# The kernel table of a state-space branch, built in four 32-column tiles by two row halves of TensorE

## The reference, cut to what matters

```
# u (T, 512) in 32 groups of 16 channels; 64 complex states per group
ab  = exp((a_re + i a_im) * dt)                  # decay of one step
bb  = f * b                                      # (group, state, 16 channels)
h_t = ab * h_(t-1) + bb u_t                      # complex
y_t = Re(c h_t) + d_skip * u_t
```

## Time and profile before

| | us |
|---|---|
| median of 3 runs | 928.42 (928.34 to 928.51) |
| span of the profiled execution, first to last instruction | 926.8 |
| TensorE busy in the span | 912.9 |
| VectorE busy in the span | 603.9 |
| ScalarE busy in the span | 442.2 |
| GpSimd busy in the span | 91.5 |

### The profile page before, as it was taken

One profiled execution on the slowest core, in us unless ns is written; L12 is line 12 of the kernel. 1 busy time (PEld: TensorE's weight loads), 2 busy tenths in 40 slices (PEclk: granted clock), 3 DMA queues, 4 the chain that ended last, 5 costly groups with the idle time before them and its releaser, 6 DMA issues.

```text
span 926.8 us, 17665 instructions
## 1 busy us (share of the span) xinstructions
PE 912.9 (98%) x7414; PEld 886.4 (96%) x7414; DVE 603.9 (65%) x815; ACT 442.2 (48%) x663; POOL 91.5 (10%) x143
## 2 busy tenths in 40 slices
PE   6999999999999999999999999999999999999998
PEld 5999999999999889999999999999999999999998
DVE  6689699511777746474568566666676666778453
ACT  7446323223776535444356544444444444446532
POOL 5390033202001210100000000000000000000000
PEclk9999999999999999999999999999999999999999
DMA  8531554824423585522223322222323222242202
GB/s 234 127 92 48 151 160 109 185 84 147 128 71 108 186 286 204 172 69 71 89 69 92 91 86 83 87 89 91 92 79 91 84 90 92 91 138 71 69 5 99
DMA packets 134694, 102.19 MB, mean 110 GB/s; under 512 B 18560, under 2 KB 124408, under 8 KB 134584
## 3 DMA queue, kind: packets, MB, share of 16 engines
q1 hardware_dynamic: 129096, 83.38, 30.5%
q0 software_dynamic: 5424, 17.65, 6.2%
q10 hardware_dynamic: 96, 0.04, 0.0%
HBM read 88.71 MB, written 12.21 MB: 109 GB/s over the span
## 4 chain that ended last, share of the span: by engine, by line
PE 92%; DVE 3%; ACT 2%; issue 1%; DMA 0%; SPq 0%; ACTq 0%; DVEq 0%
PE dense L2294 65%; PE banks L2294 20%; PE scoreA L2294 3%; PE banks L2481 2%; PE dense L2481 1%; PE scoreB L2294 1%; DVE Llo L1745 1%; ACT t L1626 1%; DVE t L2118 1%; ACT whi L1333 1%; DMA xtok<-in_x_prompt 0%; DVE Ssum L1721 0%; DVE sm L2176 0%; DVE wlo L1745 0%; ACT yh L1672 0%
## 5 line engine op out<-in xcount | busy, mean ns | idle before, releaser
L1745 DVE TENSOR_TENSOR wlo<-wraw,whi 128x1024 fp32r<-128x1024 f32 (+2 forms) x139 | 152.6, 1103 | 101.3 <-ACT whi L1333 89.0
L2294 PE MATMUL dense<-hid,whi 128*128 128x256 f32 (+1 forms) x1024 | 176.7, 294 | 0.1
L2294 PE MATMUL dense<-act_hi,whi 128*128 128x256 f32 (+1 forms) x736 | 167.4, 298 | 1.0 <-issue 0.7
L2294 PE MATMUL dense<-act_lo,whi 128*128 128x256 f32 (+1 forms) x736 | 163.3, 293 | 0.0
L2294 PE MATMUL dense<-act_hi,wlo 128*128 128x256 f32 (+1 forms) x736 | 163.3, 293 | 0.0
L2294 PEld LDWEIGHTS dense<-hid,whi 128*128 128x128 f32 x1024 | 152.5, 187 | 0.5 <-issue 0.3
L1333 ACT CAST whi<-wraw 128x1024 fp32r<-128x1024 f32 x100 | 109.9, 1101 | 45.6 <-PE banks L2294 44.1
L2294 PEld LDWEIGHTS dense<-act_hi,whi 128*128 128x128 f32 x736 | 123.4, 188 | 4.7 <-issue 3.3
L2294 PEld LDWEIGHTS dense<-act_lo,whi 128*128 128x128 f32 x736 | 124.1, 188 | 0.0
L2294 PEld LDWEIGHTS dense<-act_hi,wlo 128*128 128x128 f32 x736 | 124.0, 187 | 0.0
L2294 PE MATMUL dense<-hid,wlo 128*128 128x256 f32 (+1 forms) x512 | 108.8, 293 | 0.0
(11 more groups left out here) (367 smaller groups left out, 1590.4 us busy)
## 6 DMA issues: line engine op xcount, KB each, us to landing
wraw<-in_w_in SPq DMA_DIRECT2D x32, 512.0 KB, 5.1
wraw<-in_w_up SPq DMA_DIRECT2D x32, 512.0 KB, 4.0
wraw<-in_w_down SPq DMA_DIRECT2D x32, 512.0 KB, 3.6
gates_spill<-gst POOLq DMA_DIRECT2D x16, 288.0 KB, 3.0
page<-in_cache_k SPq DMA_DIRECT2D x16, 256.0 KB, 7.9
page<-in_cache_v SPq DMA_DIRECT2D x16, 256.0 KB, 7.3
wraw<-in_w_out SPq DMA_DIRECT2D x8, 512.0 KB, 3.7
wraw<-in_w_ple_gate SPq DMA_DIRECT2D x8, 512.0 KB, 3.6
```

The lines of the kernel that those rows point to most:

```text
L1745: return nc.vector.tensor_tensor(out=lo, in0=whole, in1=f32(hi), op=ALU.subtract)
L2294: return nc.tensor.matmul(out, lhsT, rhs, start=start, stop=stop, skip_group_check=True)
```

## The change

The table is made with more of the array at once. The four column blocks c, which before all went to partitions 0 to 15, now go to partitions 32c to 32c + 31, so that each of the four is a column tile of its own; with the two row halves for even and odd groups that makes eight tiles. A tile is 32 columns wide and the weights 16, so the weights are taken 32 wide from `bbx`, which is `bb` with 16 zero columns at either end: an even group takes its own 16 columns and the next 16, an odd group the 16 ahead and its own. The wanted 16 rows are therefore the lower ones of a tile for even groups and the upper ones for odd. `vs` becomes 128 partitions by 2 by 4 by 128, of which half the rows are used: a quarter of the elements per partition. All 64 products now fill just two banks, which ScalarE copies once each at the end (two copies in place of eight). The events are four, `("vs", x)` with 16 products each, at levels 1, 2 (two) and 3, on banks 0 and 1. `d_skip` is brought to the new layout (`dd` is 128 by 4, `same` is 1 where partition and column agree modulo 16, made by three small GpSimd additions at the start); `dti` and the addition are 128 partitions by 64 and by 128 elements instead of 16 by 512. The spill is eight transfers of 16 partitions each instead of one, all on GpSimd's queue, and `tload` waits for all eight. VectorE no longer waits for the spill in `final`.

```diff
-        for i in ((), (0, 1), (2, 3, 4, 5), (6, 7), (), ())[lvl]:
-            event("vs", i, place=2 * (i // 2 % 2) + i % 2)
+        if lvl == 1:
+            job("vs0", 0)
+            job("vs1", 1)
+        for e in ((), (0,), (1, 2), (3,), (), ())[lvl]:
+            event("vs", e)
...
-        vs = placed(9216, "vs", [GC, G, P])
+        vs = placed(9216, "vs", [P, 2, 4, P])
...
-        bb = small("bb", [P, 2, GP, GC])
+        bbx = small("bb", [P, (2 * GP + 2) * GC])
+        bb = bbx[:, GC:GC + 2 * GP * GC].rearrange("p (a g c) -> p a g c", a=2, g=GP)
...
-        dnat = placed(5640, "dnat", [G, GC])
+        dnat = placed(5640, "dnat", [4, P])
...
+            fold = GT[:, 0, 0, 0:P // 2]
+            tt(fold, ident[:, 0:P // 2], ident[:, P // 2:P], ALU.add).then_inc(count.up(pool_steps), 1)
+            pool.wait_ge(*count.last)
+            tt(fold[:, 0:32], fold[:, 0:32], fold[:, 32:64], ALU.add).then_inc(count.up(pool_steps), 1)
+            pool.wait_ge(*count.last)
+            tt(same[:, :], fold[:, 0:GC], fold[:, GC:32], ALU.add).then_inc(count.up(pool_steps), 1)
...
-                    tt(dti[:], ident[0:GC, 0:GC].unsqueeze(1).to_broadcast([GC, G, GC]),
-                       dd[:].unsqueeze(2).to_broadcast([GC, G, GC]), ALU.mult).then_inc(count.up(pool_steps), 1)
+                    tt(dti[:], same[:].unsqueeze(1).to_broadcast([P, 4, GC]),
+                       dd[:].unsqueeze(2).to_broadcast([P, 4, GC]), ALU.mult).then_inc(count.up(pool_steps), 1)
                     pool.wait_ge(*count.last)
-                    for n in (6, 7):
-                        pool.wait_ge(*read(("vs", n)))
-                    tt(vs[:, :, 0:GC], vs[:, :, 0:GC], dti[:], ALU.add).then_inc(count.up(vs_ready), 1)
+                    for odd in range(2):
+                        pool.wait_ge(*read(f"vs{odd}"))
+                    tt(vs[:, :, :, 0:GC], vs[:, :, :, 0:GC], dti[:].unsqueeze(1).to_broadcast([P, 2, 4, GC]),
+                       ALU.add).then_inc(count.up(vs_ready), 1)
                     pool.wait_ge(vs_ready, 1)
-                    pool.dma_start(vs_d, vs[:]).then_inc(vs_spilled, 16)
+                    for c in range(4):
+                        for odd in range(2):
+                            r = 32 * c + GC * odd
+                            pool.dma_start(vs_d.rearrange("h (e c o) m -> c o h e m", c=4, o=2)[c, odd],
+                                           vs[r:r + GC, odd]).then_inc(vs_spilled, 16)
...
-                    pool.wait_ge(vs_spilled, 16)
+                    pool.wait_ge(vs_spilled, 16 * 8)
...
-                    scalar.wait_ge(*full(e))
-                    if a[0] == 0:
+                    if a[0] == 3:
                         scalar.wait_ge(k_stored[0], 16 * 3)
                         scalar.wait_ge(k_stored[1], 16 * 2)
-                    g0 = 8 * (a[0] // 2)
-                    nc.scalar.copy(vs[:, g0 + a[0] % 2:g0 + 8:2, :],
-                                   bank(e)[0:GC, :].rearrange("p (a b) -> p a b", a=4)).then_inc(
-                                       count.upto(*read(e)), 1)
+                        for odd in range(2):
+                            scalar.wait_ge(*full(f"vs{odd}"))
+                            nc.scalar.copy(vs[:, odd].rearrange("p e m -> p (e m)"), bank(f"vs{odd}")).then_inc(
+                                count.upto(*read(f"vs{odd}")), 1)
...
-                    vector.wait_ge(vs_spilled, 16)
...
+                    nc.vector.memset(bbx[:, 0:GC], 0.0).then_inc(count.up(dve_steps), 1)
+                    nc.vector.memset(bbx[:, GC + 2 * GP * GC:], 0.0).then_inc(count.up(dve_steps), 1)
...
-                elif k == "vs" and a[0] % 2 == 0:
+                elif k == "vs":
...
-                    for c in range(4):
-                        for part in range(2):
+                    for part in range(2):
+                        for c in range(4):
                             for odd in range(2):
-                                g = 4 * a[0] + odd + 2 * c
+                                p = 4 * x + c
                                 r = slice(64 * odd, 64 * odd + 64)
-                                ins = mm(bank(both[odd])[0:GC, P * c:P * c + P], bb[r, part, g // 2, :],
-                                         CA[r, part, g // 2, 0:CH, :].rearrange("q k c -> q (k c)"), part == 0, part == 1)
+                                at = (part * GP + p + 1 - odd) * GC
+                                ins = mm(bank(f"vs{odd}")[32 * c:32 * c + 32, P * x:P * x + P], bbx[r, at:at + 2 * GC],
+                                         CA[r, part, p, 0:CH, :].rearrange("q k c -> q (k c)"), part == 0, part == 1)
```

More of the change, by code:

```diff
@@ L706, in build @@
         hsum = sb("hsum", [P, 8, 16])
+        same = sb("same", [P, GC])
         sb("to_line", [P, 8])
@@ L768, in build @@
         Fh = small("Fh", [P, 2, GP, 9])
-        dd = small("dd", [GC, G])
+        dd = small("dd", [P, 4])
         assert at <= 112128 + 10752, at
@@ L778, in build @@
         sst = placed(21888, "sst", [P, 2, 2 * P])
-        dti = placed(25600, "dti", [GC, G, GC])
+        dti = placed(25600, "dti", [P, 4, GC])
         vT = placed(9216, "vT", [P, AT, T])
@@ L981, in _ @@
                 (rows[65:66, 0:HD], i["g_k"]), (rows[65:66, HD:P], i["g_k"]),
-                (dnat[:, :], i["ssm_d"][0].rearrange("(g c) -> g c", c=GC)),
+                (dnat[:, :], i["ssm_d"][0].rearrange("(e x) -> e x", x=P)),
                 (bnat[:, 0], i["ssm_b_re"][0].rearrange("(p g) s c -> (g s) p c", g=2)),
@@ L2023, in _ @@
                     nc.vector.tensor_copy(gqk[:], turned[:, 64:66]).then_inc(count.up(dve_steps), 1)
-                    nc.vector.tensor_copy(dd[:], bank("s5h0")[0:GC, 2 * P + NROWS:2 * P + NROWS + G]).then_inc(
+                    nc.vector.tensor_copy(dd[:], bank("s5h0")[:, 2 * P + NROWS:2 * P + NROWS + 4]).then_inc(
                         count.up(dve_steps), 1)
@@ L2530, in _ @@
                         transpose(bank("s5h0")[:, P * c:P * c + P], snat[:, c:2 * P:2])
-                    transpose(bank("s5h0")[0:GC, 2 * P + NROWS:2 * P + NROWS + G], dnat[:, :], G)
+                    transpose(bank("s5h0")[:, 2 * P + NROWS:2 * P + NROWS + 4], dnat[:, :], 4)
                     tensor.wait_ge(ldt_wide, 1)
@@ L2581, in _ @@
                     ins.then_inc(full_of(e), 1)
-                elif k == "vs" and a[0] % 2 == 0:
[L2584 to L2588, removed]
-                    for c in range(4):
-                        for part in range(2):
+                elif k == "vs":
+                    x = a[0]
+                    if x == 0:
+                        tensor.wait_ge(ca_ready, 1)
+                        for odd in range(2):
+                            if used_before(f"vs{odd}"):
+                                tensor.wait_ge(*free(f"vs{odd}"))
+                    for part in range(2):
+                        for c in range(4):
                             for odd in range(2):
-                                g = 4 * a[0] + odd + 2 * c
+                                p = 4 * x + c
                                 r = slice(64 * odd, 64 * odd + 64)
-                                ins = mm(bank(both[odd])[0:GC, P * c:P * c + P], bb[r, part, g // 2, :],
-                                         CA[r, part, g // 2, 0:CH, :].rearrange("q k c -> q (k c)"), part == 0, part == 1)
-                                if c == 3 and part == 1:
-                                    ins.then_inc(full_of(both[odd]), 1)
+                                at = (part * GP + p + 1 - odd) * GC
+                                ins = mm(bank(f"vs{odd}")[32 * c:32 * c + 32, P * x:P * x + P], bbx[r, at:at + 2 * GC],
+                                         CA[r, part, p, 0:CH, :].rearrange("q k c -> q (k c)"), part == 0, part == 1)
+                                if x == 3 and c == 3 and part == 1:
+                                    ins.then_inc(full_of(f"vs{odd}"), 1)
                 elif k in ("kout", "vout"):
```

## The result

The changed kernel takes **931.85 us** (median of six executions, 930.11 to 932.45) against 928.46 for the kernel before, a ratio of 1.0032 with a 95% interval of 1.002 to 1.0043. It is slower by 3.4 us. The prediction said 927.0 and gave "slower" 0.05: it was wrong. The profiled execution took 931.41 us with a span of 929.4.

What follows compares the result with a forecast made beforehand. TensorE was taken as the bound, tied with VectorE at unit 18, so only VectorE's 1.50 us less 0.1 for the restart counts: span 926.8 - 1.4 = 925.4, plus 1.6 gives 927.0 us, range 926.2 to 928.9.

Steps and rivals of the forecast that it cites:

- Tiles: TensorE's table products: 32 records in about 0.5 to 0.6 us, four times; 5.0 us saved of 7.3.
- GpSimd beside VectorE: Scan 3: smaller GpSimd operations cost VectorE 0.34 us in place of 1.84, so VectorE gains 1.50 us.
- The tie at unit 18 and the restart: Before unit 18 TensorE waits from 153.1 for VectorE's split; restart takes 0.1 us off, leaving a gain of 1.4 us.
- Spill and loads: Eight spill transfers land at 157.6 to 159.8, `Tm` by 170.3 to 172.5, before `y` at 175.5; no cost.
- The rest at nothing: ScalarE's fewer copies, added GpSimd additions, VectorE memsets, the dropped wait in `final` and the gates' stores change no time.
- Rival D: TensorE's 3 us pause before unit 18 slows the array afterwards, costing 1.9 us: 928.9 us; chance 0.08.
- its sign: TensorE's products after the pause come over 0.2 us apart where they now come at 0.13.
- The sum: Whole kernel: span 926.8 - 1.4 = 925.4 us, plus 1.6 from span to median, giving 927.0 us.

Runs made afterwards that it cites:

- experiment 7: Changed kernel with `same` in a corner of an existing region and unit 18's weight split put ahead of scan 3: 923.97 us, ratio 0.9958.
- experiment 8: Kernel before with only unit 18's weight split put ahead of scan 3: 928.38 us, ratio 0.9999.
- experiment 1: Changed kernel with `same` placed in a corner of an existing region, so nothing else moves: 928.82 us, ratio 1.0001 to the kernel before.
- experiment 4: Changed kernel with `same` put ahead of the weights, so weights and activations move together: 928.59 us, ratio 0.9995 to the kernel before.
- experiment 6: Changed kernel, `same` in its original place, with twelve dummy TensorE products in the pause before unit 18: 931.0 us, ratio 1.0022.
- experiment 5: Changed kernel with `same` in an existing region and twelve dummy TensorE products in the pause before unit 18: 927.93 us, ratio 0.9992.
- experiment 2: Kernel before with only 64 bytes a partition of unused padding where the change put `same`: 932.29 us, ratio 1.0037.

## Why the prediction was wrong

**Tiles: right.** Forecast 0.5 to 0.6 us for 32 records, measured 0.60, or 19 ns a record. All 128 cost 0.60 + 1.09 + 0.60 = 2.3 us (the 1.09 for 64 from experiment 7), which is what 7.3 less the forecast saving of 5.0 leaves.

**GpSimd beside VectorE: right.** Forecast a gain of 1.50 us for VectorE; scan 3 is shorter by 9.78 - 8.17 = 1.61, and its two halves take 1072 ns each, where 1071 was forecast. The pair of GpSimd operations costs 0.10 in the `sc` products and 0.14 in the additions, against the 0.34 taken. The Trainium skill (SBUF — State Buffer, Who interferes with whom) gave 0.4 to 0.7 by its rule of the lock; the trace agrees that the small operation waits out the large one (2.08 us for 128 elements) but shows less than that cost for VectorE.

**The tie at unit 18 and the restart: right.** TensorE pauses from 153.7, where 153.1 was forecast, and `wlo` releases it. Its first pair takes 156.82 - 156.45 = 0.37 us instead of 0.26: the 0.1 that was taken. Unit 18 starts at 156.45 rather than 156.23, because scan 3 began 0.37 later than before. The delay is there already at the first scan (117.18 instead of 116.82); in the profiles of kernels with the changed tables that start lies between 116.71 and 117.41, and I did not look for a cause. Experiments 7 and 8 confirm the tie from the other side.

**Spill and loads: right.** The spill has landed by 157.61 (forecast 157.6 to 159.8), and nothing is awaited at `y`. One term was too small without harm here: the last load takes 10.3 us to land, not 8.1. It is in by about 172.2; in experiment 7, where `y` comes 4.6 us sooner, this transfer is what `y` waits for.

**"The rest at nothing": the step that failed first.** It costed every added instruction and not the added region. Where `same` was put moves the activations 64 bytes against the weights and costs **3.0 to 3.3 us** (experiments 1, 4, and 6 against 5), or 3.7 between the executions at full clock, 930.5 in the mean of two against 926.8 in that of four; the padding alone costs 3.7 in a kernel that is otherwise the one before (experiment 2). None of the rivals had it.

**Rival D at 0.08: the step that failed second.** The forecast put nothing on the pause but 0.1 us for the restart. D's price was near (1.9 us of slow running, 1.4 to decide; measured 1.3 to 1.6 in the stretch and 2.0 between executions), and so was its sign (over 0.2 us apart; records came 0.24 apart). Its chance was not: the clock fell in 18 of the 22 executions of experiments 1 and 4, and in four of six of the changed kernel. "The pause is shorter and the units before it are dense" is the reason that failed; a pause of 2.75 us was enough, right behind a stretch in which TensorE was busy for 41.19 of 41.50 us. The Trainium skill (TensorE: Matmul & The Clock Gate, HAM oscillation — how this bites in real kernels) puts the penalty of a throttled stretch at half its duration. By an estimate from that page it would be 1.7 us for 3.36; the trace has 1.45 in this stretch, and 1.56 against the 18.99 us that the same three units took with the filler (experiment 6).

**The sum closes.** 927.0 as forecast, plus 3.1 for the place, plus 2.0 for the clock is 932.1; measured 931.85. Where neither loss acts, the changed tables run in 926.1 to 927.4. One small term is off in it: the forecast added 1.6 us for what lies around the span, and the kernels with the changed tables have 2.0 to 2.1. The forecast span of 925.4 us came exactly in experiment 4 and belongs to a time of 927.4.

**What stays open.** By what rule the distance between the split weights and the activations makes a block slow or fast: shifts of 32, 64 and 128 bytes cost 7.5, 3.7 and 1.0 us, a common shift nothing, and I tried no others. No run moved the weights' slots one by one, or the small constants without the weights. Why the filler gives back 0.9 us and not 2.0: its three units take 19.24, as in the undisturbed execution of experiment 4, but from `y` to the end its profiled execution needs 926.1 - 175.91 = 750.2 us instead of 925.4 - 175.90 = 749.5. All of that lies between `y` and 419 us (243.3 instead of 242.6), in code that the filler does not touch, and its cause is not known. And why one of the six executions of experiment 7 took 927.43 with a clock of 0.996.

## What to carry to other kernels

A new small region ahead of large ones is an edit to every instruction that reads them: put it where it moves nothing, or compare with padding of the same size in the kernel before, which takes one run. When a stage's work is cut and the next one waits for another engine, the saving turns into a pause. Price the pause's clock as well, and look first for an order in which the pause doesn't arise: here one moved split turned 928.8 into 924.0 us, a version 0.4% faster than the kernel before.

## What the runs showed of the hardware that was not expected

- The rate of fp32r products at a full granted clock changes with the distance between their two operands in SBUF: the same 96 records take 12.64, 12.80 or 12.82 us, and 32 unused bytes slow a kernel of 928.9 us by 7.5. Where both operands move together, no padding changes the time (4.58 us for the first block of `y`).
- A pause of 2.75 to 2.84 us can halve the granted clock, and does not always: 3.36 us at 1.2 GHz, beginning 1.4 us after the restart in one profile, about as long but beginning 0.4 us before the restart in another (experiment 1), and not at all in a third (experiment 4).
- Eight tiles of 64 rows by 32 columns at once bring a record with 128 moving columns to 19 ns, where two tiles of 16 columns took 57 and four column tiles 28.
- The time outside the span is 2.0 to 2.1 us in each profiled kernel with the changed tables and 1.7 to 1.8 in each one without. I know no reason.
